# Ten early places instead of eight for the key and value cache, two of them in the space of transposed k

## The chip, the cores and the metric

The kernel runs on one core of a Trainium2 chip. The metric is device time in microseconds of one launch. A second number, the span, is the time from the first to the last instruction in a profiled execution.

## What is computed

One layer of a decoder in float32, for a prompt of 1024 tokens and for 8 sequences that each get 4 new tokens behind 2048 cached ones. Only the part on the sampled sequences matters here: attention of their 4 new tokens over the cached keys and values, with three dilations whose windows are (128,1), (512,4) and (2048,16).

```python
k_all = jnp.concatenate([k_buf.astype(k.dtype), k], axis=1)
v_all = jnp.concatenate([v_buf.astype(v.dtype), v], axis=1)
stats = [dilated_branch_sample(q, k_all, v_all, w, d) for w, d in DILATED_CFG]
...
mixed = jnp.concatenate([rms_norm(y_a, g_norm_a), rms_norm(y_b, g_norm_b)], axis=-1) @ w_out
```

For a sequence this touches the last 512 cached rows (the near keys) and 4 of every 16 rows of the first 1536 (the far keys), and its own 4 rows. After it come an output projection, a layer norm and a mixture of experts.

## The kernel before

The stages run one after the other, each in a block of its own with a barrier at the end: front, attention (the prompt's), sampling, mixing (normalisation and output projection), experts, finish. Buffers are placed by hand at addresses, and every order is written out by hand with semaphores; each engine runs its own list.

In `attention`, SyncE first loads modulation weights, then the first eight pieces of the cache: four near pieces of k into ring0["slots"] (L1104), four far ones into ring0["far"] (L1110), between copies of the cache to the output (L1089). Its last waits, at the end of its list, are for those copies and for the modulation rows in DRAM (L1120, L1121).

In `sampling`, eight sequences are taken in two groups g of four. The cache comes in 32 pieces: 16 of k, then 16 of v. In each 16 the order is group 0 near (4 sequences), group 0 far, group 1 near, group 1 far. A near piece is 1 MB (128 partitions, 8 KB each), a far piece 0.75 MB (96 partitions, 8 KB each, from rows 32 KB apart). They go round a ring of RING = 10 places; piece n goes to place n % 10 once the reader of piece n - 10 has passed (`consumed`). Places 0 to 7 are ring0's, 8 and 9 are ring1. SyncE issues them in order (`load`, L1415 near, L1417 far).

TensorE has 16 units u of k, eight per group (units 0 to 3 and 8 to 11 are near, the others far). For each unit it turns k (`turn`, L1456), in two halves that ScalarE and VectorE copy out of PSUM (`evict`), then makes the scores of the unit before (`scores`, L1470). The own keys come last in a group (`own_scores`). VectorE masks a group (`mask`, L1625), ScalarE takes the exponential, TensorE turns the weights (`turn_weights`), and sums the values (`values`, L1512): part 0 of a group uses near pieces, part 1 far ones. `select` (L1526) gathers the result. In between, VectorE and ScalarE normalise the prompt's rows (`row_sums`, `scale`, `lower`, `upper`), which split them in a high and a low half for the output projection. When the ring's pieces in places 2 and 3 have been read for the last time, SyncE loads half of w_out over them (L1431); `mixing` loads the other half as its first DMA (L1856).

The order of the last part of TensorE's list:

```python
values(0, 0)
for r in range(3):
    turn_weights(1, r)
values(0, 1)
values(1, 0)
select(0)
values(1, 1)
select(1)
```

Of the kernel before, what the change touches and what calls it, by code (L numbers as in the profile page):

```python
# [23 lines left out]
F32 = mybir.dt.float32  # L24
# [6 lines left out]
P = 128  # L31
D = 1024
KD = D // P
SEQ = 1024
# [101 lines left out]
def program(nc, a, out, dram):  # L136
    ctx = ExitStack()
    with ctx:
# [6 lines left out]
        silu = sb("silu", [P, KD, NSEQ])  # L145
        s_ring0 = [Sem(nc.alloc_semaphore(f"ring{j}"), 16) for j in range(8)]
        s_wo = [Sem(nc.alloc_semaphore(f"wo{j}"), 16) for j in range(4)]
# [5 lines left out]
        with ExitStack() as late:  # L153
            sbl = alloc(late)
            at_a = aligned(nc.sbuf_base)
            gelu_in = sbl("gelu_in", [P, CT, TOK])
            ssq = sbl("ssq", [P, NT + 1, CT])
            with ExitStack() as c2:
                sb2 = alloc(c2)
                at_q = aligned(nc.sbuf_base)  # L160
                qT = sb2("qT", [P, PAIRS, TOK])
                kT = sb2("kT", [P, PAIRS, TOK])
                at_v = aligned(nc.sbuf_base)
                v = sb2("v", [P, NT + 1, DB])
                front(nc, a, out, dram, ident, cols, silu, gelu_in, ssq, qT, kT, v, at_q, at_v, s_cache)
                at_b = aligned(nc.sbuf_base)
                ybT = sb2("ybT", [P, PAIRS, TOK])
                at_r = aligned(nc.sbuf_base)
                ring0 = {"at": at_r, "slots": sb2("ring0", [P, 4, 4, DB]),
                         "at_far": aligned(nc.sbuf_base), "far": sb2("ring_far", [P, 4, 4, DB]),  # L170
                         "wo": nc.alloc_sbuf_tensor_at("wo_early", [P, 4, D], F32, offset=at_r + 2 * 16 * DB)}
                attention(nc, a, out, dram, ident, silu, qT, kT, v, ybT, ring0, s_ring0)
                split = {n: nc.alloc_sbuf_tensor_at(n, [P, CT, TOK], F32R, offset=at)
                         for n, at in (("yah", at_q), ("ybh", at_q + 4 * CT * TOK), ("yal", at_a), ("ybl", at_b))}
                sampling(nc, a, ident, qT, kT, v, gelu_in, ybT, ssq, at_v, split, ring0, s_ring0, s_wo)
                mixing(nc, a, out, dram, ident, cols, gelu_in, ybT, ssq, logits, at_v, split, ring0, s_wo, s_rows)
# [839 lines left out]

def attention(nc, a, out, dram, ident, silu, qT, kT, v_all, ybT, ring0, s_ring0):

# [7 lines left out]
    with ExitStack() as ctx:  # L1026
# [22 lines left out]
        s_cp = S("a_cp", 16)  # L1049
        s_cT = S("a_cT")  # L1050
        s_mw = [S(f"a_mw{p}", 16) for p in range(RING)]
        s_mb = S("a_mb", 16)
# [30 lines left out]
        def _(sp):  # L1083
# [36 lines left out]
            sp.wait_ge(s_cp.sem, s_cp.at(B - CT + 2))  # L1120
            sp.wait_ge(s_mo.sem, s_mo.at(GROUPS * QUAD))  # L1121

        @block.gpsimd
        def _(pool):
            nc.gpsimd.memset(mbias[:, :, :], 0.0).then_inc(s_mz.sem, s_mz.unit)
            nc.gpsimd.memset(cT[:, :, :], 0.0).then_inc(s_cT.sem, s_cT.unit)
            pool.wait_ge(s_cT.sem, s_cT.at(1))
            nc.gpsimd.tensor_copy(cT[:, :, 0:NSEQ], silu[:, :, :]).then_inc(s_cT.sem, s_cT.unit)

        @block.tensor  # L1130
# [179 lines left out]

def sampling(nc, a, ident, qT, kT, v_all, ya, ybT, ssq, at_v, split, ring0, s_ring0, s_wo):

    G = B // 4
    KT_ = 8
    RING = 10
    PIECES = 8 * 2 * G
    NPC = 4 * 2 * G
    NW = 4
    with ExitStack() as ctx:
# [4 lines left out]
        S = lambda n, unit=1: Sem(new_sem(n), unit)  # L1324
        ring1 = sb("s_ring", [P, RING - 8, 4, DB])
        wo = ring0["wo"]
# [3 lines left out]
        qz = sb("s_qz", [P, B, PAIRS, NS])  # L1330
        kown = sb("s_kown", [P, PAIRS, NS])
        bias = sb("s_bias", [P, SKEYS])
# [17 lines left out]
        s_b = S("s_b", 16)  # L1350
        s_ring = [*s_ring0, *(S(f"s_r{j}", 16) for j in range(8, RING))]
        s_z = S("s_z")
        s_q = S("s_q")
        s_own = S("s_ownc")
        s_tp = S("s_tp")
# [33 lines left out]
        ROUNDS = ((0, 1, 2, 3), (4, 5, 6, 7), (8,))  # L1389
        early = (ring0["slots"], ring0["far"], ring1)  # L1390
        slot = lambda n: early[n % RING // 4][:, n % RING % 4, :, :]
        k_piece = lambda g, h, c: 8 * g + 4 * h + c
# [13 lines left out]
        @block.sync  # L1406
        def _(sp):
            sp.dma_start(bias[:, :], a["k_sbias"][:, 0, :]).then_inc(s_b.sem, s_b.unit)

            def load(n):  # L1410
                if n >= RING:
                    s, value = consumed(n - RING)
                    sp.wait_ge(s.sem, s.at(value))
                if n // 4 % 2 == 0:
                    sp.dma_start(slot(n), rows_of(n)[PAST - NEAR:PAST, :].rearrange("(p i) n -> p i n", i=4)).then_inc(s_ring[n % RING].sem, s_ring[n % RING].unit)  # L1415
                else:
                    sp.dma_start(slot(n)[0:FARM], rows_of(n)[0:PAST - NEAR, :].rearrange("(m i) n -> m i n", i=16)[:, 0:4, :]).then_inc(s_ring[n % RING].sem, s_ring[n % RING].unit)  # L1417

            for n in range(8, PIECES):
                if n == 8:  # L1420
                    sp.dma_start(own[:, :], a["k_own"]).then_inc(s_in.sem, s_in.unit)
                    sp.dma_start(sel[:, :, :], a["k_sel"]).then_inc(s_in.sem, s_in.unit)
                if n == 18:
                    sp.wait_ge(s_lg.sem, s_lg.at(1))
                    sp.dma_start(bias[:, :], a["k_sbias"][:, 1, :]).then_inc(s_b.sem, s_b.unit)
                load(n)
            s, value = consumed(v_piece(0, 1, 3))
            sp.wait_ge(s.sem, s.at(value))
            w = a["w_out"].rearrange("(k p) n -> p k n", p=P)
            for i in range(NW):  # L1430
                sp.dma_start(wo[:, i, :], w[:, CT + i, :]).then_inc(s_wo[i].sem, s_wo[i].unit)  # L1431
# [12 lines left out]
        def _(pe):  # L1444
# [29 lines left out]
            def own_scores(g):  # L1474
                pe.wait_ge(s_own.sem, s_own.at(1))
                lo = SKEYS - NS
# [95 lines left out]
        def _(act):  # L1572
# [7 lines left out]
            def upper(x, c):  # L1580
                act.wait_ge(s_ma.sem, s_ma.at(2 * CT * x + 2 * c + 2))
                if x == 0 and c == 0:
                    act.wait_ge(s_q.sem, s_q.at(1))
                    act.wait_ge(s_own.sem, s_own.at(1))
                src, dst = ((ya, yah), (ybT, ybh))[x]
                nc.scalar.copy(dst[:, c, 0:SEQ], src[:, c, 0:SEQ]).then_inc(s_hi.sem, s_hi.unit)

            nc.scalar.copy(kown[:, :, :], kT[:, :, SEQ:TOK]).then_inc(s_own.sem, s_own.unit)
            for u in range(KT_ * G):
# [20 lines left out]
        def _(v):  # L1610
# [92 lines left out]
            for u in range(KT_ * G):  # L1703
# [3 lines left out]
                if 2 <= u <= 4:  # L1707
                    add_squares(u - 2)
                if 5 <= u < 5 + CT:
                    scale(0, u - 5, first)  # L1710
                if u == KT_:
                    row_sums(1)
                    mask(0)
                if KT_ + 1 <= u < KT_ + 1 + CT:
                    lower(0, u - KT_ - 1)
                if u == KT_ + 2:
# [1295 lines left out]
```

## Time and profile before

| what | us |
|---|---|
| median of 3 runs | 1340.67 |
| lowest and highest run | 1338.21, 1344.5 |
| the profiled execution | 1340.65 |
| its span | 1338.7 |
| TensorE busy (matmul) | 1196.7 (89% of the span) |
| VectorE busy | 733.9 (55%) |
| ScalarE busy | 576.5 (43%) |
| sampling stage, from its first instruction to the next stage's | 491.7 to 591.1 |

TensorE is the busiest engine over the whole span. The share is a mean over stages with different limits, so for one stage windows, timelines and DMA landings have to be read. PE is TensorE, DVE VectorE, ACT ScalarE, POOL GpSimd, SPq the queue of SyncE. PEclk is the granted clock of TensorE as a share of full speed.

### The profile page before, as it was taken

What the parts mean: (1) busy time and instruction counts of PE and PEld (TensorE: products, weight loads), DVE (VectorE), ACT (ScalarE), POOL (GpSimd) and SP (SyncE); (2) the same over time, 40 slices, a digit from 0 to 9 for tenths busy, and PEclk for the clock granted to TensorE, in tenths of its full rate; (3) what the DMA queues carried; (4) which work ended last, traced back from release to release, by engine and by line L of the source; (5) the groups of instructions that cost most, each with busy time, mean ns of one, the idle gap of its engine ahead of it and who ended that gap; (6) DMA issues with size and microseconds to landing.
All of it is one profiled execution on the core that took longest, in us unless ns stands there. A gap on an engine that the chain in (4) does not pass through costs nothing. (4 is left out here: it accounts for less than half of the span.)

```text
span 1338.7 us, 20995 instructions
## 1 busy us (share of the span) xinstructions
PE 1196.7 (89%) x6981; PEld 905.5 (68%) x6982; DVE 733.9 (55%) x1248; ACT 576.5 (43%) x845; POOL 136.1 (10%) x128
## 2 busy tenths in 40 slices
PE   5999899999799988779993499999999999999885
PEld 3799777876355667337872377787778877777751
DVE  3457524433456756435545685789641454477237
ACT  3655532111355554222333165687531454466124
POOL 0000000000000000003331200011000000001055
PEclk8999889999899999879996599999999999999987
DMA  9998921269769948975325585999661355698464
GB/s 336 363 321 282 331 71 58 79 206 313 275 221 374 321 154 272 295 216 178 123 100 190 181 322 217 359 384 387 230 238 63 120 216 213 235 329 311 178 248 161
DMA packets 102029, 316.95 MB, mean 237 GB/s; under 512 B 12845, under 2 KB 21533, under 8 KB 95290
## 3 DMA queue, kind: packets, MB, share of 16 engines
q1 hardware_dynamic: 85354, 274.25, 58.7%
q0 software_dynamic: 6432, 23.33, 4.8%
q10 hardware_dynamic: 10176, 18.49, 3.7%
q8 instruction: 41, 0.67, 0.2%
q14 instruction: 26, 0.21, 0.0%
HBM read 281.22 MB, written 101.93 MB: 286 GB/s over the span
## 5 line engine op out<-in xcount | busy, mean ns | idle before, releaser
L2621 DVE TENSOR_TENSOR e_downl<-e_wd,e_downh 128x1024 fp32r<-128x1024 f32 x64 | 74.1, 1219 | 62.5 <-ACT e_downh L2516 62.5
L2688 PE MATMUL e_psY<-e_downh,e_hTh 128*128 128x512 f32 x216 | 91.9, 426 | 15.9 <-DVE e_hTl L2642 10.2
L2516 ACT CAST e_downh<-e_wd 128x1024 fp32r<-128x1024 f32 x64 | 62.4, 1046 | 64.6 <-DMA e_wd<-in_w_exp_down 64.4
L571 PE MATMUL n_psA<-n_wh,u_h 128*128 128x512 f32 (+1 forms) x216 | 88.2, 408 | 0.4 <-DVE n_wl L835 0.4
L2688 PE MATMUL e_psG<-e_gateh,e_xTh 128*128 128x512 f32 x216 | 86.5, 400 | 2.0 <-DVE e_gatel L2615 2.0
L2688 PE MATMUL e_psG<-e_uph,e_xTh 128*128 128x512 f32 x216 | 87.8, 406 | 0.2 <-issue 0.2
L2689 PE MATMUL e_psY<-e_downh,e_hTl 128*128 128x512 f32 x216 | 86.7, 402 | 0.0
L2690 PE MATMUL e_psY<-e_downl,e_hTh 128*128 128x512 f32 x216 | 86.6, 401 | 0.0
L573 PE MATMUL n_psA<-n_wh,u_l 128*128 128x512 f32 (+1 forms) x216 | 85.9, 398 | 0.0
L2689 PE MATMUL e_psG<-e_gateh,e_xTl 128*128 128x512 f32 x216 | 85.9, 398 | 0.0
L2690 PE MATMUL e_psG<-e_gatel,e_xTh 128*128 128x512 f32 x216 | 85.9, 398 | 0.0
L572 PE MATMUL n_psA<-n_wl,u_h 128*128 128x512 f32 (+1 forms) x216 | 85.5, 396 | 0.0
L2689 PE MATMUL e_psG<-e_uph,e_xTl 128*128 128x512 f32 x216 | 85.3, 395 | 0.0
L2690 PE MATMUL e_psG<-e_upl,e_xTh 128*128 128x512 f32 x216 | 85.3, 395 | 0.0
L2615 DVE TENSOR_TENSOR e_gatel<-e_wg,e_gateh 128x1024 fp32r<-128x1024 f32 x64 | 74.1, 1220 | 17.0 <-ACT e_gateh L2509 17.0
L2521 ACT CAST e_xTh<-e_psT 128x512 fp32r<-128x512 f32 x56 | 32.7, 585 | 112.5 <-PE e_psT L2683 106.7
L2615 DVE TENSOR_TENSOR e_upl<-e_wu,e_uph 128x1024 fp32r<-128x1024 f32 x64 | 74.0, 1217 | 0.6 <-ACT e_uph L2509 0.5
L2509 ACT CAST e_gateh<-e_wg 128x1024 fp32r<-128x1024 f32 x64 | 62.3, 1047 | 13.2 <-issue 13.2
L2626 DVE TENSOR_TENSOR e_xTl<-e_psT,e_xTh 128x512 fp32r<-128x512 f32 x56 | 38.6, 688 | 48.6 <-ACT e_xTh L2521 48.6
L2509 ACT CAST e_uph<-e_wu 128x1024 fp32r<-128x1024 f32 x64 | 62.4, 1049 | 5.6 <-DMA e_wu<-in_w_exp_up 5.5
L2688 PEld LDWEIGHTS e_psY<-e_downh,e_hTh 128*128 128x128 f32 x216 | 41.6, 193 | 26.4 <-DVE e_downl L2621 13.7
L2589 POOL COPY e_ids<-ids 128x1 int32 (+1 forms) x28 | 15.6, 556 | 416.3 <-PE e_psT L2683 412.0
(417 smaller groups left out, 2600.0 us busy)
## 6 DMA issues: line engine op xcount, KB each, us to landing
e_wg<-in_w_exp_gate SPq DMA_DIRECT2D x16, 2048.0 KB
e_wu<-in_w_exp_up SPq DMA_DIRECT2D x16, 2048.0 KB
e_wd<-in_w_exp_down SPq DMA_DIRECT2D x16, 2048.0 KB, 14.9
out_k_s<-in_cache_win_k SPq DMA_DIRECT2D x8, 4088.0 KB, 24.1
out_v_s<-in_cache_win_v SPq DMA_DIRECT2D x8, 4088.0 KB, 34.0
a_wring<-in_w_ada SPq DMA_DIRECT2D x16, 1024.0 KB, 5.2
scratch_y<-e_y ACTq DMA_DIRECT2D x54, 256.0 KB, 5.6
n_wr<-in_w_in SPq DMA_DIRECT2D x20, 512.0 KB, 10.6
```

The source lines that it names most:

```text
L571: nc.tensor.matmul(dst, lh, rh, start=(k == 0), stop=False)
L572: nc.tensor.matmul(dst, lh, rl, start=False, stop=False)
L573: last = nc.tensor.matmul(dst, ll, rh, start=False, stop=(k == KD - 1))
L2509: nc.scalar.copy(w[name][H_][:, k:k + 2, :], ew[name][:, k:k + 2, :]).then_inc(s_wh.sem, s_wh.unit)
L2516: nc.scalar.copy(w["down"][H_][:, k, :], ew["down"][:, k, :]).then_inc(s_dh.sem, s_dh.unit)
L2521: nc.scalar.copy(xT[H_][:, par, 4 * half:4 * half + 4, :], psT[:, :, :]).then_inc(s_xh.sem, s_xh.unit)
L2615: nc.vector.tensor_tensor(w[name][L_][:, 2 * i:2 * i + 2, :], ew[name][:, 2 * i:2 * i + 2, :], w[name][H_][:, 2 * i:2 * i + 2, :], ALU.sub ...
L2621: nc.vector.tensor_tensor(w["down"][L_][:, k, :], ew["down"][:, k, :], w["down"][H_][:, k, :], ALU.subtract).then_inc(s_dl.sem, s_dl.unit)
L2626: nc.vector.tensor_tensor(xT[L_][:, par, blocks, :], psT[:, :, :], xT[H_][:, par, blocks, :], ALU.subtract).then_inc(s_tc.sem, s_tc.unit)
L2688: nc.tensor.matmul(dst, left[H_], right[H_], start=first, stop=False)
L2689: nc.tensor.matmul(dst, left[L_], right[H_], start=False, stop=False)
L2690: return nc.tensor.matmul(dst, left[H_], right[L_], start=False, stop=last)
```

## The change

The ring has 12 places. Places 8 and 9 lie in the space of kT, the transposed keys of the prompt, which nobody reads after the attention's last scores; each takes two of its four pairs. Pieces 8 and 9 (k of group 1, near) are loaded at the end of SyncE's list in the attention, each behind a wait on the scores that read that half of kT. The own keys, which sampling needs of kT, are copied to a buffer k_own by GpSimd in the attention, not by ScalarE in sampling. Places 10 and 11 are the old ring1. The high half of the attention's rows (ybh) is written to the same space as places 8 and 9, so the first of its casts waits for the value pieces there. w_out waits for a later reader, since places 2 and 3 now end with pieces 26 and 27. On VectorE, the first mask goes ahead of the row sums, the fourth scaling of the first half moves from unit 8 to unit 9, and the four subtractions start one unit later.

```diff
@@ attention @@
+            sp.wait_ge(s_kown.sem, s_kown.at(1))
+            for i in range(2):
+                sp.wait_ge(s_s.sem, s_s.at(2 * chunk0[STEPS // 2 * (i + 1)]))
+                rows = a["cache_win_k"][4 + i].rearrange("s h d -> s (h d)")[PAST - NEAR:PAST, :]
+                sp.dma_start(ring0["in_k"][i][:, :, :], rows.rearrange("(p i) n -> p i n", i=4)).then_inc(s_ring0[8 + i].sem, s_ring0[8 + i].unit)
...
+            nc.gpsimd.tensor_copy(kown[:, :, :], kT[:, :, SEQ:TOK]).then_inc(s_kown.sem, s_kown.unit)
@@ sampling @@
-    RING = 10
+    RING = 12
...
-            for n in range(8, PIECES):
-                if n == 8:
+            for n in range(10, PIECES):
+                if n == 10:
...
-                if n == 18:
+                if n == 20:
                     sp.wait_ge(s_lg.sem, s_lg.at(1))
...
-            s, value = consumed(v_piece(0, 1, 3))
+            s, value = consumed(v_piece(1, 0, 3))
             sp.wait_ge(s.sem, s.at(value))
...
-                    act.wait_ge(s_own.sem, s_own.at(1))
+                if x == 1 and c == 0:
+                    act.wait_ge(s_pv.sem, s_pv.at(2))
...
-            nc.scalar.copy(kown[:, :, :], kT[:, :, SEQ:TOK]).then_inc(s_own.sem, s_own.unit)
...
-                if 5 <= u < 5 + CT:
-                    scale(0, u - 5, first)
                 if u == KT_:
+                    mask(0)
                     row_sums(1)
-                    mask(0)
-                if KT_ + 1 <= u < KT_ + 1 + CT:
-                    lower(0, u - KT_ - 1)
+                if u in (5, 6, 7, 9):
+                    scale(0, (5, 6, 7, 9).index(u), first)
+                if KT_ + 2 <= u < KT_ + 2 + CT:
+                    lower(0, u - KT_ - 2)
```

## Rows read from the trace of the kernel before

**Rows 1.** Windows: length, busy us (count) of each engine, PEclk, DMA share, GB/s

```profile
480.00:490.00 10.00, 7.87 (x105) 6.77 (x101) 3.22 (x8) 3.43 (x8) 0.00 (x0) 1.00 0.01 2
...
562.00:578.00 16.00, 10.22 (x42) 2.59 (x40) 3.68 (x5) 0.00 (x0) 0.00 (x0) 0.79 1.01 219
...
566.00:570.00 4.00, 3.62 (x20) 0.99 (x24) 0.00 (x0) 0.00 (x0) 0.00 (x0) 0.50 1.04 225
```

**Rows 2.** Timeline of PE in sampling: start, us, instruction, idle before and its releaser

```profile
522.77 0.63 PE L1470 MATMUL s_psS<-s_kTs,s_qz 128*32 128x128 f32 x13 [0.97 <-DVE s_mn L1625]
525.69 0.84 PE L1470 MATMUL s_psS<-s_kTs,s_qz 128*32 128x128 f32 x19 [2.28 <-issue]
...
546.80 0.25 PE L1479 MATMUL s_psS<-s_kown,s_qz 128*32 128x32 f32 x2 [2.81 <-issue]
...
555.27 3.64 PE L1512 MATMUL s_psO<-ring,s_pT 96*32 96x512 f32 x32
...
561.77 1.05 PE L1512 MATMUL s_psS<-ring_far,s_kTs 128*32 128x512 f32 x2 [0.89 <-DMA ring_far<-in_cache_win_v]
566.38 6.36 PE L1512 MATMUL s_psS<-ring_far,s_kTs 128*32 128x512 f32 x26 [3.56 <-DMA ring_far<-in_cache_win_v]
...
580.34 1.06 PE L1512 MATMUL s_psS<-ring,s_kTs 96*32 96x512 f32 x1 [2.33 <-DMA ring<-in_cache_win_v]
...
588.48 1.47 PE L1526 MATMUL s_psS<-s_sel,s_om 128*128 128x32 f32 x8 [0.94 <-DVE s_om L1681]
```

**Rows 3.** Issues of pieces 14-15, then 22-23: ns and start us, us to landing

```profile
L1417 SPq DMA_DIRECT2D ring_far<-in_cache_win_k x2: 312/368/425, 515.1 to 515.4; - x2
DMA to landing us min/median/max: 5.8/7.9/10.0
...
L1417 SPq DMA_DIRECT2D ring<-in_cache_win_v x2: 312/370/427, 541.1 to 541.5; - x2
DMA to landing us min/median/max: 10.0/11.5/13.0
```

**Rows 4.** The same of pieces 24-25, 26-27, 28-31, and SPq's issue at unit 11

```profile
L1415 SPq DMA_DIRECT2D ring_far<-in_cache_win_v x2: 427/428/430, 542.0 to 542.4; - x2
DMA to landing us min/median/max: 14.8/15.8/16.8
...
L1415 SPq DMA_DIRECT2D ring_far<-in_cache_win_v x2: 328/380/433, 554.3 to 554.6; - x2
DMA to landing us min/median/max: 7.5/9.6/11.7
...
L1417 SPq DMA_DIRECT2D s_ring<-in_cache_win_v x2: 428/428/428, 555.1 to 555.6; - x2
L1417 SPq DMA_DIRECT2D ring<-in_cache_win_v x2: 312/370/428, 559.0 to 559.3; - x2
...
DMA to landing us min/median/max: 14.8/17.9/21.0
...
530.93 0.80 SPq L1415 DMA_DIRECT2D s_ring<-in_cache_win_v  x2
```

**Rows 5.** SyncE's last wait in the attention, and the last scores there

```profile
L1121 SPq EVENT_SEMAPHORE  x1: 17/17/17, 480.6 to 480.6; - x1
...
473.80 1.13 PE L1140 MATMUL a_psS<-kT,qT 64*128 64x512 f32 x4
```

**Rows 6.** Timelines of SPq and ACT around the end of sampling

```profile
559.80 1.85 SPq L1431 DMA_DIRECT2D wo_early<-in_w_out  x4
591.14 1.75 SPq L1856 DMA_DIRECT2D x_wo_rest<-in_w_out  x4
...
555.75 3.88 ACT L1586 CAST ybh<-ybT 128x1024 fp32r<-128x1024 f32 x4
```

**Rows 7.** Timeline of DVE: the last subtraction of the first half, unit 15's eviction

```profile
535.59 1.22 DVE L1672 TENSOR_TENSOR yal<-gelu_in,yah 128x1024 fp32r<-128x1024 f32 x1
...
541.80 0.96 DVE L1618 COPY s_kTs<-s_psK 128x768 f32<-128x768 f32 x1 [1.31 <-PE s_psK L1456]
```

More of the change, by code:

```diff
@@ L145, in program @@
         silu = sb("silu", [P, KD, NSEQ])
-        s_ring0 = [Sem(nc.alloc_semaphore(f"ring{j}"), 16) for j in range(8)]
+        s_ring0 = [Sem(nc.alloc_semaphore(f"ring{j}"), 16) for j in range(10)]
         s_wo = [Sem(nc.alloc_semaphore(f"wo{j}"), 16) for j in range(4)]
@@ L165, in program @@
                 front(nc, a, out, dram, ident, cols, silu, gelu_in, ssq, qT, kT, v, at_q, at_v, s_cache)
+                at_k = at_q + 4 * PAIRS * TOK
+                kown = sb2("k_own", [P, PAIRS, NS])
                 at_b = aligned(nc.sbuf_base)
@@ L170, in program @@
                          "at_far": aligned(nc.sbuf_base), "far": sb2("ring_far", [P, 4, 4, DB]),
-                         "wo": nc.alloc_sbuf_tensor_at("wo_early", [P, 4, D], F32, offset=at_r + 2 * 16 * DB)}
-                attention(nc, a, out, dram, ident, silu, qT, kT, v, ybT, ring0, s_ring0)
+                         "wo": nc.alloc_sbuf_tensor_at("wo_early", [P, 4, D], F32, offset=at_r + 2 * 16 * DB),
+                         "in_k": [nc.alloc_sbuf_tensor_at(f"ring_k{i}", [P, 4, DB], F32, offset=at_k + 2 * i * 4 * TOK) for i in range(2)]}
+                attention(nc, a, out, dram, ident, silu, qT, kT, kown, v, ybT, ring0, s_ring0)
                 split = {n: nc.alloc_sbuf_tensor_at(n, [P, CT, TOK], F32R, offset=at)
                          for n, at in (("yah", at_q), ("ybh", at_q + 4 * CT * TOK), ("yal", at_a), ("ybl", at_b))}
-                sampling(nc, a, ident, qT, kT, v, gelu_in, ybT, ssq, at_v, split, ring0, s_ring0, s_wo)
+                sampling(nc, a, ident, qT, kown, v, gelu_in, ybT, ssq, at_v, split, ring0, s_ring0, s_wo)
                 mixing(nc, a, out, dram, ident, cols, gelu_in, ybT, ssq, logits, at_v, split, ring0, s_wo, s_rows)
@@ L1015, in _, with attention @@
                     nc.vector.tensor_copy(strow[:, :], psX[0:NTAIL, :]).then_inc(s_tr.sem, s_tr.unit)
-def attention(nc, a, out, dram, ident, silu, qT, kT, v_all, ybT, ring0, s_ring0):
+def attention(nc, a, out, dram, ident, silu, qT, kT, kown, v_all, ybT, ring0, s_ring0):
     FIRST = 2 * D // MW
@@ L1050, in attention @@
         s_cT = S("a_cT")
+        s_kown = S("a_kown")
         s_mw = [S(f"a_mw{p}", 16) for p in range(RING)]
@@ L1308, in _, with sampling @@
             divisor(STEPS - 1)
-def sampling(nc, a, ident, qT, kT, v_all, ya, ybT, ssq, at_v, split, ring0, s_ring0, s_wo):
+def sampling(nc, a, ident, qT, kown, v_all, ya, ybT, ssq, at_v, split, ring0, s_ring0, s_wo):
     G = B // 4
     KT_ = 8
-    RING = 10
+    RING = 12
     PIECES = 8 * 2 * G
@@ L1324, in sampling @@
         S = lambda n, unit=1: Sem(new_sem(n), unit)
-        ring1 = sb("s_ring", [P, RING - 8, 4, DB])
+        ring1 = sb("s_ring", [P, RING - 10, 4, DB])
         wo = ring0["wo"]
@@ L1350, in sampling @@
         s_b = S("s_b", 16)
-        s_ring = [*s_ring0, *(S(f"s_r{j}", 16) for j in range(8, RING))]
+        s_ring = [*s_ring0, *(S(f"s_r{j}", 16) for j in range(10, RING))]
         s_z = S("s_z")
         s_q = S("s_q")
-        s_own = S("s_ownc")
         s_tp = S("s_tp")
@@ L1389, in sampling @@
         ROUNDS = ((0, 1, 2, 3), (4, 5, 6, 7), (8,))
-        early = (ring0["slots"], ring0["far"], ring1)
-        slot = lambda n: early[n % RING // 4][:, n % RING % 4, :, :]
+        places = [*(ring0["slots"][:, i, :, :] for i in range(4)), *(ring0["far"][:, i, :, :] for i in range(4)),
+                  *(r[:, :, :] for r in ring0["in_k"]), *(ring1[:, i, :, :] for i in range(RING - 10))]
+        slot = lambda n: places[n % RING]
         k_piece = lambda g, h, c: 8 * g + 4 * h + c
@@ L1474, in own_scores @@
             def own_scores(g):
-                pe.wait_ge(s_own.sem, s_own.at(1))
                 lo = SKEYS - NS
```

1 line of the change is left out of this document (removed).

## The prediction, made before the change was run

> **What bounds the kernel now.** The table of engines and the forty slices say that TensorE is busy nearly everywhere. The change lies in one stage, sampling, so I cut the span into short windows around it [rows 1]. Two things stand out. From 480 to 490 us, the last ten microseconds of the attention, the DMA engines do nothing (share 0.01, 2 GB/s). From 562 to 578 us they are full (1.01) and TensorE works 10.22 of 16 us. Then I read TensorE's own timeline there [rows 2]: from 559.8 us on it sums the values of the second group of four sequences, and stops four times for a piece of the cache; the rows show 0.89, 3.56 and, as the last, 2.33 us. That one ends at 580.34, when piece 31, the last of 32, lands. What follows it is a fixed tail: the rest of the products, the sums of the last block, a scaling on VectorE, the selecting product at 588.48, and the next stage's first DMA at 591.14, 10.8 us in all [rows 2, 6]. So the landing of piece 31 sets the end of the stage, and everything later waits for it.
>
> Next I asked what sets that landing. The landing times of the pieces give it [rows 3, 4]. A piece lands at its issue plus its time to landing: 22 and 23 at 551.1 and 554.5, 24 and 25 at 556.8 and 559.2, 26 and 27 at 561.8 and 566.3, 28 at 569.9 and 31 at 580.3. They come one after another without a pause, so the queue is the bound and not the issue. The steps show two prices. A near piece (1 MB, 128 partitions) behind another costs 2.4 us. A far piece (0.75 MB in 96 partitions) costs 3.4 to 3.6, though it is smaller: (580.3 - 569.9) / 3 = 3.5. A near piece with far ones behind it costs 566.3 - 561.8 = 4.5.
>
> **The change part by part.**
>
> *Two more places in the space of k.* Pieces 8 and 9 are issued in the attention, behind everything that SyncE has there. SyncE leaves its last wait at 480.6 us and the last scores that read k run at 473.8 to 474.9 [rows 5], so neither of the two added waits on the scores, nor that on the copy, holds it. The first lands like one on an idle queue, at most 5.8 us (that of a far piece [rows 3]), the second a near step of 2.4 later: by 489, inside the idle stretch and ahead of sampling at 491.7. Cover: that stretch; without it they would cost the 4.8 us that they cost now.
>
> *All later loads go two pieces earlier.* Each piece n now waits for what piece n - 12 held. Pieces 12 to 15 are issued near 502, 16 to 19 near 515, 20 to 23 when unit 11 has been turned, 24 to 27 when unit 15 has been turned, 28 to 31 when the first half of the first group's values is done. In the trace these moments are 530.9, 541.1 to 542.0 and 554.3 [rows 3, 4]. The queue has by 530.9 nothing left: 12 to 15, four far pieces, take it to 502 + 5.8 + 4.5 + 2 x 3.4 = 519, and 16 to 19 need 4 x 2.4 us more. From there I add up. Far pieces 20 to 23: 5.8 us for the first on an idle queue, 4.5 for the second (515.4 + 10.0 less 515.1 + 5.8), and 3.4 each for two more [rows 3]: 548.0. Near pieces 24 to 27, issued well before that: 3 x 2.4 + 4.5 = 11.7, so 559.7. Far pieces 28 to 31, issued before that too: 3.6 + 3 x 3.5 = 14.1, so 573.8. That is 6.5 us ahead of 580.3. Bounds: with every far piece at 3.4 and every near one at 2.4, 530.9 + 5.8 + 3 x 3.4 + 4 x 2.4 + 4 x 3.4 = 570.1, a gain of 10.2. If only the transfer of two near pieces leaves the busy stretch, 2 x 2.4 = 4.8. I take 6.5, because it uses for each neighbour of pieces the step of the same pair in the trace.
>
> TensorE reaches the last four pieces earlier, so it does not become the bound: values of the second group begin about 559.8 as now (558.9, where the rows' products end, and those of the new tokens) and no longer stop: 3.64 us for 32 products, as the group from 555.27 shows [rows 2]. The selecting product takes about 1, and from 564.5 on it waits for pieces 29, 30, 31. That wait is longer than the present ones, so the clock is again at its lower level (0.50 from 566 to 570, after a stop of 3.56 us [rows 1, 2]) and the tail stays 10.8 us.
>
> *Weights w_out.* They reuse places 2 and 3, which now hold pieces 26 and 27, so their four DMAs wait for the second group's near values: about 563.5 instead of 559.8 [rows 6]. They stand behind piece 31 in the queue anyway: 2 MB are two near pieces, 4.8 us, so they land at 578.6. The next stage needs them at 591.5 - 6.5 = 585. Zero, with 6 us of margin. If it were late, each microsecond would count whole.
>
> *The copy of k's own columns* leaves ScalarE, where a wait for TensorE followed it, for an idle GpSimd early in the attention: zero, at worst some tenths.
>
> *ybh written into k's space.* ScalarE's four casts, 3.88 us from 555.75 [rows 6], must wait for values that end at 558.9, so they end at 562.8. Two of VectorE's four subtractions (1.22 us each [rows 7]) follow, then the first group's result near 565, then the other two: about 567.5, before the last products. Zero; cover is the wait for piece 31.
>
> *Mask before row sums, one scaling later.* In unit 8 VectorE masks earlier. TensorE waited 0.97 us for it at 522.77, so 1.0 is the most that can come. But 13 products later it stands for 2.28 us with nothing that the profile shows as a reason [rows 2]. I read both this and the 2.81 us ahead of 546.80 as waits for instructions. If so, an earlier arrival is waited away. I take 0 of 0 to 1.0. In unit 13 VectorE gets one more subtraction of 1.22 us, with only 1.31 us of slack by unit 15 [rows 7]; the turn of unit 15 may slip 0.6 to 1.0 us. The loads that hang on it stand in a queue full until 548, so zero.
>
> The Trainium skill weighs on two of these steps, and the sum does not use it. By "DMA: Bandwidth & Descriptors", section "Bandwidth", 16 MB move at 425 GB/s. The near pieces agree (1 MB in 2.4 us), the far ones don't (0.75 MB in 3.5 us). By that rate a far piece would cost an estimated 1.9 us and the queue would never bind again. That is the first rival below, and the rows speak against it. "Runtime: NRT & Kernel Launch", section "Instruction fetch mechanics", says that instructions come by DMA in blocks of 256 and that this is mostly hidden. The trace has two unexplained waits of 2.3 and 2.8 us where the DMA engines are full, so here it isn't hidden. The second and third rivals rest on the rows for it.
>
> Sum: -6.5 us of 1340.65 (profiled execution; span 1338.7, median of the runs 1340.67): 1334.1.
>
> **Rivals.** *The queue is faster than I say.* Piece 31 lands at 570.1 and TensorE's clock stays high: 10.2, and the tail is shorter: its products take 7.2 us now (580.34 to 588.48 less 0.94) and at full clock about 3.64 less the four made ahead, with 0.9 for the new tokens, 4.1; selecting some 0.4 less. Together 10.2 + 3.1 + 0.4 = 13.7, 1327.0. For it: the 3.4 and 2.4 are measured. Against: every stretch with near and far pieces mixed shows more. Without any DMA bound the values would end near 569 and the stage near 572.5, 18.6 earlier, 1322. 12% for both.
>
> *Instruction waits eat it.* The queue now is four pieces deep where it was two, and before 530.9 it is full in stretches where it was not. A wait of 2.3 to 2.8 more, once or twice before unit 11 is turned, moves the whole chain of loads: gain 1 to 4, 1338. For it: the two waits seen [rows 2]; against: their number depends on where block ends fall. 23%.
>
> *Slower.* The same mechanism at each block of instructions between 491.7 and 530.9, about four: 4 x 2.8 = 11.2 against 6.5, so 4.7 slower, 1345.4. It decides from the third wait on (8.4 over 6.5), and with low clock behind each wait (3.1 us a half of values) passes 0.5%. 7% for slower at all, 5% past 0.5%.
>
> *It does nothing,* because the loads in the attention are not issued before its end, or the queue was not the limit: 1340.7. The 480.6 [rows 5] and the landings without a pause [rows 4] speak against. 5%.
>
> **How the numbers follow.** The forecast has 53%. Its own range is 1332 to 1337. The range of 8 in 10 takes in the bound of 10.2 with 1.0 from the mask (11.2, 1329.5) and some scatter of the runs below it, the instruction waits and the case of no effect above. It leaves out the first rival (12%) and the slower one (7%): 1328.5 to 1341.0. About 0.5%, 6.7 us, can be told from no change. That line lies inside my forecast, so it splits it: faster by more 47% (a little over half of the forecast's 53%, the first rival, and the part of the steps with 1.0 from the mask), within 48%, slower 5%.
>
> **What would show it.** Right: pieces 8 and 9 issued at 480.7 and landed by 488; 20 to 23 issued near 531 and all landed near 548; no stop of TensorE in the second group's near values; piece 31 at 573 to 575; the next stage's first DMA near 584.6 with w_out there since 579; the rest of the kernel shifted as a whole. Wrong: unexplained waits of TensorE before 531 longer than 2.3 us in sum, far pieces landing 4 us apart, or a later stage that gives the time back.

## The result and the profile after

| | before | changed |
|---|---|---|
| median of 9 runs each | 1340.67 us | 1328.3 us |
| lowest to highest | 1335.45 to 1344.5 | 1324.19 to 1333.6 |
| ratio, 95% interval | | 0.992, 0.99 to 0.9941 |
| profiled execution, its span | 1340.65, 1338.7 | 1328.28, 1326.3 |

The change makes the kernel 0.8% faster, 10.7 us by the ratio, where 6.5 was forecast. The first question is whether that time comes from sampling. I cut each span at the first DMA of each stage, as SyncE's timeline shows them:

| us | up to attention | attention | sampling | mixing | experts | finish | span |
|---|---|---|---|---|---|---|---|
| before | 339.0 | 152.7 | 99.4 | 130.3 | 560.8 | 56.5 | 1338.7 |
| changed | 338.2 | 155.1 | 88.9 | 130.4 | 557.3 | 56.3 | 1326.3 |

Sampling gives 10.5. The rest nearly cancels (-0.8, +2.4, +0.1, -3.5, -0.2), and it is scatter: over the 14 profiled kernels of this study the attention took 151.7 to 156.1 us and the experts 556.7 to 560.8, in no order that fits their edits. So I read only the stage, and in time from its own start: 491.7 us before [rows 1 to 6], 493.35 changed. (Lengths of stages and parts are differences of times rounded to 0.1 us, so their last digit can be off by one.)

SyncE's timeline of the changed kernel in sampling (start, us, instruction, tiles, count):

```profile
483.39 0.83 SPq L1130 DMA_DIRECT2D ring_k<-in_cache_win_k  x2
493.35 0.33 SPq L1417 DMA_DIRECT2D s_bias<-in_k_sbias  x1
...
530.36 0.80 SPq L1426 DMA_DIRECT2D ring_k<-in_cache_win_v  x2
...
542.20 1.77 SPq L1424 DMA_DIRECT2D ring<-in_cache_win_v  x4
552.42 1.74 SPq L1426 DMA_DIRECT2D ring_far<-in_cache_win_v  x4
561.73 1.77 SPq L1440 DMA_DIRECT2D wo_early<-in_w_out  x4
582.28 1.75 SPq L1864 DMA_DIRECT2D x_wo_rest<-in_w_out  x4
```

The first line is the new one, pieces 8 and 9. Unit 11's release (530.36) answers to 530.93 in [rows 4], the last line to 591.14 in [rows 6]. The landings of pieces 8-9, 20-21, 22-23, 24-27 and 28-31 (ns of the issues, their starts, then us to landing):

```profile
L1130 SPq DMA_DIRECT2D ring_k<-in_cache_win_k x2: 368/396/423, 483.4 to 483.8; - x2
DMA to landing us min/median/max: 4.9/5.9/6.9
...
L1426 SPq DMA_DIRECT2D ring_k<-in_cache_win_v x2: 328/378/427, 530.4 to 530.7; - x2
DMA to landing us min/median/max: 5.7/7.0/8.3
...
L1426 SPq DMA_DIRECT2D s_ring<-in_cache_win_v x2: 393/616/838, 531.2 to 531.7; - x2
DMA to landing us min/median/max: 12.2/13.5/14.8
...
L1424 SPq DMA_DIRECT2D ring<-in_cache_win_v x4: 346/430/435, 542.2 to 543.5; - x4
DMA to landing us min/median/max: 6.5/9.8/14.5
...
L1426 SPq DMA_DIRECT2D ring_far<-in_cache_win_v x4: 328/424/426, 552.4 to 553.7; - x4
DMA to landing us min/median/max: 8.9/13.2/17.7
```

Start plus time to landing: pieces 8 and 9 are there at 488.3 and 490.7, before the stage starts. Piece 23 lands at 531.7 + 14.8 = 546.5, piece 27 at 543.5 + 14.5 = 558.0 and piece 31 at 553.7 + 17.7 = 571.4, where it was 580.3 [rows 4]. TensorE's timeline of the changed kernel, with the same columns and the idle time before in brackets:

```profile
525.11 0.85 PE L1479 MATMUL s_psS<-s_kTs,s_qz 128*32 128x128 f32 x19 [1.00 <-issue]
...
540.76 0.60 PE L1479 MATMUL s_psS<-s_kTs,s_qz 128*32 128x96 f32 x17 [1.38 <-issue]
...
546.60 0.25 PE L1487 MATMUL s_psS<-k_own,s_qz 128*32 128x32 f32 x2 [1.54 <-issue]
...
564.60 1.04 PE L1520 MATMUL s_psS<-ring_far,s_kTs 96*32 96x512 f32 x2 [0.92 <-DMA ring_far<-in_cache_win_v]
567.86 1.92 PE L1520 MATMUL s_psS<-ring_far,s_kTs 96*32 96x512 f32 x2 [2.22 <-DMA ring_far<-in_cache_win_v]
571.46 6.38 PE L1520 MATMUL s_psS<-ring_far,s_kTs 96*32 96x512 f32 x26 [1.69 <-DMA ring_far<-in_cache_win_v]
...
579.77 1.31 PE L1534 MATMUL s_psS<-s_sel,s_om 128*128 128x32 f32 x8 [0.94 <-DVE s_om L1689]
```

These answer to [rows 2]. The 0.97 for the mask is gone, and 2.28 and 2.81 with nothing as their reason are now 1.00 and 1.54, with a new one of 1.38. All three waits for data are for far pieces, 3.3 to 3.6 us apart; the near values no longer stop. The chain is as before: TensorE waits for the landing of the last piece, and from there to the next stage it takes 582.28 - 571.46 = 10.8 us, the same 10.8.

| us | before | changed |
|---|---|---|
| stage start to unit 11's release | 39.2 | 37.0 |
| release to the first use of piece 31 | 49.4 | 41.1 |
| to the next stage's first DMA | 10.8 | 10.8 |

### The profile page after: what moved, and what is told of

Read it like the earlier page. It is cut to its first block and busy times, and to the rows that moved or that the text cites. A ratio compares the mean times of both kernels' runs of the same rounds, so it can differ in the third digit from the quotient of the medians.

```text
span 1326.3 us, 20996 instructions
## 1 busy us (share of the span) xinstructions
PE 1191.3 (90%) x6981; PEld 903.1 (68%) x6982; DVE 735.7 (55%) x1248; ACT 575.8 (43%) x844; POOL 135.3 (10%) x129
## 5 line engine op out<-in xcount | busy, mean ns | idle before, releaser
L2696 PE MATMUL e_psY<-e_downh,e_hTh 128*128 128x512 f32 x216 | 90.9, 421 | 14.3 <-DVE e_hTl L2650 9.7
L2517 ACT CAST e_gateh<-e_wg 128x1024 fp32r<-128x1024 f32 x64 | 62.4, 1047 | 13.2 <-issue 13.2
L1223 DVE CUSTOM_DVE_ANT_0 lg<-a_psS,bias 128x512 f32<-128x512 f32 (+3 forms) x96 | 49.3, 551 | 13.8 <-DMA bias<-in_k_bias 11.3
## 6 DMA issues: line engine op xcount, KB each, us to landing
n_wr<-in_w_in SPq DMA_DIRECT2D x20, 512.0 KB, 10.6
```

What stands on the lines that cost most here:

```text
L1223: nc.vector.tensor_tensor_reduce(out=lg[:, s % 3, hh, 512 * c:512 * c + m], in0=psS[:, hh, k % 2, 0:m], in1=bias[:, lo:lo + m], scale=-0.1 ...
L2517: nc.scalar.copy(w[name][H_][:, k:k + 2, :], ew[name][:, k:k + 2, :]).then_inc(s_wh.sem, s_wh.unit)
L2696: nc.tensor.matmul(dst, left[H_], right[H_], start=first, stop=False)
```

## Experiments

The parts can be separated: the order on VectorE, the two places, and the loads in the attention. Times with an interval are ratios to the kernel before on the same chip, with the 95% interval. Four kernels ran only once and have a time alone, beside the median of the kernel before on their chip. Stage lengths are from one profile each. In the diffs `...` stands for lines left out, and the `.then_inc(...)` behind a DMA is left out too.

**The order alone** (before, with only the lines of VectorE's order changed):

```diff
                 if u == KT_:
+                    mask(0)
                     row_sums(1)
-                    mask(0)
...
-                    scale(0, u - 5, first)
+                    scale(0, (5, 6, 7, 9).index(u), first)
```

> The kernel before with only VectorE's new order (mask ahead of row sums, fourth scaling one unit later). The sampling stage took 99.4 us before and 89.0 after. Queue theory: the loads that TensorE releases at unit 11 may come up to 1.0 us earlier, by the wait for the mask that goes; piece 31 still ends the stage, so the stage takes 98.4 to 99.4 us. Rival, that the order brings all of the 2.3 us by which the release came earlier: 97.1 us. Device time 1338 to 1340.7.

Ratio 0.9998 (0.9976 to 1.002), stage 102.5 us. TensorE's timeline of this kernel:

```profile
524.83 1.49 PE L1470 MATMUL s_psS<-s_kTs,s_qz 128*32 128x128 f32 x19 [3.87 <-issue]
```

The mask's 0.97 is gone and the unexplained wait is 3.87 where it was 2.28: what arrived earlier was waited away, and TensorE goes on 34.4 us into the stage, where it was 34.0 before. The clock in the 6 us from 524 on was 0.52. That makes this profile's stage longer than the 98.4 to 99.4 expected; the total doesn't show it. The order buys nothing by itself.

**Everything but the order** (changed kernel with the old order):

```diff
                 if u == KT_:
-                    mask(0)
                     row_sums(1)
+                    mask(0)
```

> The changed kernel with VectorE's old order. Queue theory: the stretch from the release at unit 11 to the landing of piece 31 stays 41 us (49.4 before), the release comes 0 to 2.3 us later than in the changed kernel: stage 89.0 to 91.3 us, device time 1328 to 1331. Rival, that the order matters more than the places: stage over 93 us.

Ratio 0.9925 (0.9902 to 0.9947), stage 88.8. That is the whole gain without the order. Its TensorE shows the mask's wait again and no stop of the other kind in that unit:

```profile
523.34 1.31 PE L1479 MATMUL s_psS<-s_kTs,s_qz 128*32 128x128 f32 x32 [0.97 <-DVE s_mn L1633]
```

Unit 11 is released 529.05 - 492.2 = 36.9 us into the stage, as in the changed kernel. So the 2.2 us won before unit 11 aren't the order's either. Behind the release piece 31 takes the 41.1 us that it takes in the changed kernel.

**The early load alone** (changed kernel, but each later piece n waits again for what piece n - 10 held):

```diff
-    RING = 12
+    RING = 10
...
+        slot = lambda n: ring0["in_k"][n - 8][:, :, :] if n in (8, 9) else places[n % RING]
```

> The changed kernel, but with a ring of 10 as before: pieces 8 and 9 are loaded into the space of k in the attention, and pieces 18, 19, 28, 29 go to the old ring1, each behind the same reader as before. Queue theory: the queue still has two near and eight far and four more near pieces to load behind unit 11, so the early load by itself gives nothing: stage 97 to 99.4 us. Rival, that the transfer taken out of the stage is what helps, wherever it was: 4.8 us, 94.6 or less, down to 89.

Ratio 0.9997 (0.9976 to 1.0018), stage 97.6. Unit 11 is released 37.2 us in, and the use of piece 31 comes 49.6 after it, as before. **The places alone** (pieces 8 and 9 loaded in sampling):

```diff
-            for i in range(2):
-                sp.wait_ge(s_s.sem, s_s.at(2 * chunk0[STEPS // 2 * (i + 1)]))
...
-            for n in range(10, PIECES):
-                if n == 10:
+            for n in range(8, PIECES):
+                if n == 8:
```

> The changed kernel, but pieces 8 and 9 are issued as sampling's first pieces and not in the attention; the 12 places stay. Queue theory: 4.8 us more of transfers stand ahead of piece 12, the queue has no idle stretch left before unit 11, and piece 31 lands 2.5 to 4.8 us later than in the changed kernel: stage 91.5 to 93.8 us. Rival, that only the number of places counts: 89 us.

Ratio 0.9942 (0.9918 to 0.9967), stage 93.3: release 39.9 in, piece 31 used 43.6 later. By the ratios the early load alone is worth 0.4 us, the places alone 7.8, and both without the order 10.0; by the stages 1.8, 6.1 and 10.6. The places carry it. What the early load adds to them, 2.3 us by the ratios, is inside the intervals; the stages show it in two parts.

The first part lies behind the release. In places alone piece 31 is used 2.5 us later behind it than in the changed kernel, because the queue hasn't run dry when unit 11 releases the next loads. The windows around the release, changed and then places alone (length, busy us and count of each engine, clock, DMA share, GB/s):

```profile
530.00:531.00 1.00, 1.00 (x11) 0.96 (x9) 0.85 (x2) 0.64 (x1) 0.00 (x0) 1.00 0.08 27
...
532.00:534.00 2.00, 2.00 (x37) 1.80 (x30) 2.00 (x3) 0.75 (x1) 0.00 (x0) 1.00 1.03 425
```

Pieces 20 and 21 land 5.7 and 8.3 us behind their issue in the first, 8.3 and 11.2 in the second. The second part lies ahead of the release. Release of unit 11 in us into the stage:

| without the early load | | with it | |
|---|---|---|---|
| before | 39.2 | changed | 37.0 |
| order alone | 41.9 | all but the order | 36.9 |
| places alone | 39.9 | early load alone | 37.2 |

The stops of TensorE in that stretch differ. Before has waits of 0.97 and 2.28, the order alone 3.87, the early load alone 0.18. Places alone has only 1.13 but a low clock without a stop ahead of it, as its window shows:

```profile
516.00:522.00 6.00, 6.00 (x62) 5.42 (x62) 2.56 (x4) 1.74 (x2) 0.00 (x0) 0.56 1.03 217
```

Seven of the 14 kernels have such a stretch, between 22 and 30 us into the stage. In warm_tail (below), whose instructions are the changed kernel's up to there, it stands from 516.74 to 520.74 at 0.57:

```profile
516.74:520.74 4.00, 4.00 (x47) 3.47 (x47) 2.15 (x3) 1.56 (x3) 0.00 (x0) 0.57 0.88 324
```

It has no stop where the changed kernel has 1.22 us of them, but TensorE is busy for 35.8 us up to the release instead of 34.7, and the release comes at 36.9 against 37.0. far_contig gives 36.7. So the eight releases fall in two groups, by the early load. It isn't the only way: before_wide (below), which has no early load but shorter far transfers, has its release at 36.2. far_split, which has the early load and twice as many far transfers, has it at 37.9. What the groups have in common is in the next experiment.

**Are the unexplained waits tied to a place in TensorE's list?** The changed kernel with 64 waits, all met long before, ahead of unit 0:

```diff
+            for _ in range(64):
+                pe.wait_ge(s_ring[0].sem, s_ring[0].at(1))
             for u in range(KT_ * G):
```

> The changed kernel with 64 more waits, already met, in TensorE's list ahead of sampling's first unit. If the unexplained stops of TensorE (0.22, 1.00, 1.38, 1.54 us, behind 15, 13, 15 and 30 products of their blocks) are waits for the next block of instructions, they move by 64 instructions, 32 products with their weight loads, to earlier places in the list. Rival, that they hang on data or semaphores: they stay behind the same products. Time within 2 us of the changed kernel either way.

One run: 1332.52 us (before's median there 1339.32), stage 93.4. TensorE's stops without a reason are now these, and no others:

```profile
496.60 6.33 PE L1465 MATMUL s_psK<-ident,ring 128*128 128x128 f32 x32 [5.09 <-issue]
...
543.78 0.32 PE L1465 MATMUL s_psK<-ident,ring 96*128 96x96 f32 x1 [2.42 <-issue]
```

The stops among the scores and at the new tokens are gone, although data, buffers and the other engines' lists are the same; one stands now inside a turn. (The first holds the added waits themselves, so its 5.09 can't be taken as a price.) The two stops ahead of the release prove little, since they are missing in warm_tail as well. But the three behind it, 1.38, 0.30 and 1.54, stand in warm_tail with the same lengths at the same products, and here all three are gone. So the stops hang on positions in the instruction list. Behind the stop of 2.42 the clock was 0.50 for the window from 544 to 548. The time was expected within 2 us of the changed kernel; one run can't settle that, but the stage is 4.5 us longer. Its release comes 2.9 us later, behind the added waits, and the queue is then full, as in places alone (share 1.07 from 532 to 534), so piece 31 is used 43.7 us behind it.

That they are waits for instructions another view of the traces shows. The DMA queues have one of kind "instruction", with transfers of 16 KB; the view by queue places each in time. Three windows of 0.1 us, from 523.2 in before, 522.8 in the changed kernel and 517.3 in far_wide (packets, MB, share of 16 engines):

```profile
q8 instruction: 1, 0.02, 71.3%
...
q8 instruction: 1, 0.02, 58.6%
...
q8 instruction: 1, 0.02, 68.1%
```

Before's transfer takes 1.13 us to 524.4, and the stop of 2.28 ends at 525.69. The changed kernel's takes 0.95 us to 523.8, and the stop of 1.00 ends at 525.11. Over the 14 kernels there are 28 stops with the releaser "issue" besides those of 0.30 and the 5.09, and each ends 1.3 to 1.7 us after such a transfer has ended. (The stops of 0.30, always ahead of the same scores, have none that close.) The trace doesn't say whose instructions these are; the 28 matches say that they are TensorE's. The transfers take 0.9 to 1.4 us; what makes a stop long is that one starts late. The transfer that the two stops above wait for, in us into the stage:

| | start of the transfer |
|---|---|
| before, order alone, places alone | 31.6, 31.8, 32.3 |
| changed, all but the order, early load alone, warm_tail | 29.5, 29.3, 29.4, 29.3 |
| far_contig, far_split, 64 waits ahead | 27.1, 30.2, 30.9 |
| before_wide, far_128, far_wide, wide_warm | 24.2 each |

The changed kernel, warm_tail and far_128 have the same list of TensorE up to there and have run it without a stop up to 24.2 us. So the start depends on what else the DMA engines carry. With the early load the transfer starts 2.1 us sooner than before, and that is the 2.2 us of the release but for 0.1. That also is why the order buys nothing: the stop ends when the instructions are there, whenever TensorE gets to it. How a queue of cache pieces holds the transfer up no run here shows.

**Why does a far piece cost 3.5 us?** The prediction took this price as given, and piece 31 hangs on it. Theory: its runs of 8 KB lie 32 KB apart. Rival: it goes to 96 partitions, not 128. Two kernels read other rows of the cache for the far pieces, first in 96 partitions without gaps:

```diff
-rows_of(n)[0:PAST - NEAR, :].rearrange("(m i) n -> m i n", i=16)[:, 0:4, :]
+rows_of(n)[0:4 * FARM, :].rearrange("(m i) n -> m i n", i=4)
```

> The changed kernel, but each far piece is read from the first 384 cached rows in one contiguous stretch (still 96 partitions of 8 KB each), so it attends to other keys and values than it should. If a far piece costs 3.3 to 3.5 us because its rows lie 32 KB apart, it now costs about 1.8 (three quarters of a near piece), the queue no longer binds and TensorE doesn't stop for values: stage 79 to 82 us. Rival, that the 96 partitions cost it: far pieces still land 3.3 us apart, stage 89 us.

Then in 128 partitions with gaps, 1 MB instead of 0.75:

```diff
-sp.dma_start(slot(n)[0:FARM], rows_of(n)[0:PAST - NEAR, :].rearrange("(m i) n -> m i n", i=16)[:, 0:4, :])
+sp.dma_start(slot(n), rows_of(n)[0:PAST - NEAR, :].rearrange("(m i) n -> m i n", i=12)[:, 0:4, :])
```

> The changed kernel, but each far piece is read as 128 partitions of 8 KB whose rows lie 24 KB apart (1 MB instead of 0.75), so the keys and values are others than they should be. If the distance costs: 4/3 of 3.4 us, 4.5 us a piece, piece 31 lands some 9 us later, stage 97 us. Rival, that 96 partitions are the cost: 2.4 us a piece as for near ones, stage 80 to 84 us.

Issue and landing of pieces 28-31 in the first, then in the second:

```profile
L1426 SPq DMA_DIRECT2D ring_far<-in_cache_win_v x4: 328/425/426, 554.1 to 555.4; - x4
DMA to landing us min/median/max: 9.0/13.9/18.8
```

```profile
L1426 SPq DMA_DIRECT2D ring_far<-in_cache_win_v x4: 328/430/431, 549.4 to 550.7; - x4
DMA to landing us min/median/max: 7.3/10.6/13.9
```

From the first to the last landing, by three: (574.2 - 563.1) / 3 = 3.7 us without gaps, (564.6 - 556.7) / 3 = 2.6 with gaps and a third more bytes. The theory fell; the partitions are the price. Nor is it the smaller transfer: w_out's four of 0.5 MB, to 128 partitions, stand behind piece 31 in the changed kernel and land 1.3 us apart ((576.3 - 572.4) / 3):

```profile
L1440 SPq DMA_DIRECT2D wo_early<-in_w_out x4: 347/432/434, 561.7 to 563.1; - x4
DMA to landing us min/median/max: 10.7/12.0/13.2
```

Why 96 partitions cost more no run here shows. The stages are 89.9 and 81.1, the times of one run each 1329.93 and 1322.51 (before's median there 1339.32). The window of the second kernel in the middle of these landings:

```profile
560.00:564.00 4.00, 1.60 (x6) 0.14 (x2) 2.25 (x3) 0.00 (x0) 0.00 (x0) 0.95 1.00 416
```

Share 1.00 at 416 GB/s, where it is 1.01 at 219 in [rows 1]. So the share says that the engines are occupied, not how much they move.

**Far pieces in 128 partitions with the right rows.** The last 32 partitions take rows that nobody uses:

```diff
-sp.dma_start(slot(n)[0:FARM], rows_of(n)[0:PAST - NEAR, :].rearrange("(m i) n -> m i n", i=16)[:, 0:4, :])
+sp.dma_start(slot(n), rows_of(n).rearrange("(m i) n -> m i n", i=16)[:, 0:4, :])
```

> The changed kernel, but each far piece that sampling loads is read from all 2048 cached rows, 4 of every 16, in 128 partitions of 8 KB: 1 MB instead of 0.75, the last 32 partitions unused, result unchanged. If the 96 partitions are what makes a far piece slow (3.3 to 3.5 us), it now costs 2.4 to 2.6: 12 pieces from unit 11 on take about 33 us instead of 41, stage 81 to 82 us, device time about 1320. Rival, that the larger transfer costs more than the shape saves: stage 89 or more.

Ratio 0.9861 (0.983 to 0.9893), median 1319.35 beside 1336.24 of before on that chip: the lowest ratio here, 1.4% against the change's 0.8%. Stage 83.6, where 81 to 82 was expected.

```profile
L1426 SPq DMA_DIRECT2D ring_far<-in_cache_win_v x4: 327/430/431, 549.7 to 551.1; - x4
DMA to landing us min/median/max: 7.2/11.0/14.8
...
565.87 6.46 PE L1520 MATMUL s_psS<-ring_far,s_kTs 96*32 96x512 f32 x26 [1.46 <-DMA ring_far<-in_cache_win_v]
...
543.91 0.25 PE L1487 MATMUL s_psS<-k_own,s_qz 128*32 128x32 f32 x2 [0.50 <-issue]
```

3.0 us a piece, more than the 2.4 to 2.6 expected, and of the waits with no releaser only 0.30 and 0.50 are left. **The same edit in the kernel before:**

> The kernel before with far pieces in 128 partitions. Queue theory: the loads behind unit 11 (14 pieces) take about 38 us instead of 49, now partly bound by their issue times (pieces 30 and 31 are issued 28 us behind unit 11), so piece 31 lands 10 to 12 us earlier: stage 87 to 89.5 us, device time 1328 to 1331. So the shape alone would be worth about what the change was. Rival, that the change took the same slack and the shape works only with 12 places: stage over 94 us.

Ratio 0.9913 (0.9881 to 0.9945), stage 87.7, piece 31 used 567.93 - 527.33 = 40.6 us after unit 11's release. The shape alone is worth what the whole change is worth: both shorten the same queue. The two together give 1.4%; whether that is less than 0.9 and 0.8 added the intervals don't tell.

**Far pieces in two parts, 64 and 32 partitions:**

```diff
...
+                    for part in (slice(0, 64), slice(64, FARM)):
+                        sp.dma_start(slot(n)[part], rows[part, 0:4, :])
```

> The changed kernel with each far piece that sampling loads in two DMAs, of 64 and of 32 partitions. If a DMA over 96 partitions is slow by the way in which that number is spread, 64 and 32 should go at the near pieces' rate, 0.75 x 2.4 = 1.8 to 2.5 us a piece, stage 80 to 82 us. Rival, that any transfer to fewer than 128 partitions is slow: still 3.3 us a piece or more, stage 89 us.

```profile
L1429 SPq DMA_DIRECT2D ring_far<-in_cache_win_v x8: 471/528/584, 555.3 to 559.2; - x8
DMA to landing us min/median/max: 6.5/11.3/17.0
```

1332.5 us in one run (before's median there 1336.24), stage 93.6; piece 31 is used at 576.31, 45.0 us behind the release, where the changed kernel has 41.1. The first of the eight lands at 561.8 at the earliest and the last at 576.2: no cheaper than whole. The Trainium skill, "DMA: Bandwidth & Descriptors", section "Rules for kernel authors", asks for 128 partitions and 1 MiB or more per DMA for full bandwidth, and says that two transfers to disjoint halves of the partitions serialize. The 128 partitions agree with these kernels (2.6 to 3.0 us against 3.4 to 3.7); the size doesn't show here, since w_out's 0.5 MB move at about the near pieces' rate. The split into 64 and 32 isn't one in halves, but is no quicker either.

**The tail at full clock.** The 26 products behind piece 31 take 6.38 us, and the window from 572 to 576 shows a clock of 0.50. Idle products fill the waits for pieces 29 to 31:

```diff
+            def warm(n):
+                pe.wait_ge(s_ma.sem, s_ma.at(16))
+                for _ in range(n):
+                    nc.tensor.matmul(psK[:, 0, 0, :], ident[:, :], ident[:, :], start=True, stop=True)
...
+                                if g == 1 and part == 1 and c >= 1:
+                                    warm((6, 11, 12)[c - 1])
```

> The changed kernel with 6, 11 and 12 idle products of 128 columns into free PSUM ahead of TensorE's waits for pieces 29, 30 and 31. If the tail behind piece 31 is long because the clock has fallen (0.50), the time from its landing to the next stage's first DMA falls from 10.8 to about 7.3 us, and the next stage's first products run at full clock too: stage 85.5 us and 2 to 3 us more behind it, device time 1322 to 1325. Rival, that the clock falls all the same or the idle products only delay: stage 89 to 90 us, device time as the changed kernel's or 1 us more.

Ratio 0.9919 (0.989 to 0.9949), stage 87.0, where 85.5 was expected. Its TensorE, one timeline line and two windows:

```profile
571.78 3.62 PE L1527 MATMUL s_psS<-ring_far,s_kTs 96*32 96x512 f32 x26
...
568.00:572.00 4.00, 4.00 (x31) 2.98 (x34) 0.00 (x0) 0.00 (x0) 0.00 (x0) 1.00 0.96 289
...
580.00:584.00 4.00, 1.95 (x11) 1.66 (x12) 2.73 (x3) 4.00 (x5) 0.29 (x2) 0.50 0.81 273
```

The products take 3.62 instead of 6.38, and the tail 579.72 - 571.78 = 7.9 us instead of 10.8 (7.3 expected). At the passage to the next stage the clock is at 0.50 again. The total doesn't show the 2 us of the stage against the changed kernel: the intervals of 0.992 and 0.9919 are wider than that. **Both, with wide far pieces and 2, 10 and 10 idle products** (far_wide's edit, `warm` as above, and other numbers):

```diff
+                                    warm((2, 10, 10)[c - 1])
```

> Far pieces in 128 partitions and 2, 10 and 10 idle products ahead of the waits for pieces 29, 30 and 31 in the changed kernel. The tail behind piece 31 ran at the low clock with far pieces of 128 partitions too (26 products in 6.50 us); at the high clock it is 2.9 us shorter: stage 78 to 79 us, device time about 1317.5. Rival, that the idle products now delay the real ones: stage 81 us or more.

Ratio 0.9882 (0.9847 to 0.9917), stage 83.7: no better than wide alone.

```profile
L1426 SPq DMA_DIRECT2D ring_far<-in_cache_win_v x4: 328/430/432, 546.6 to 547.9; - x4
DMA to landing us min/median/max: 7.0/10.7/14.3
...
559.29 2.50 PE L1509 MATMUL s_psK<-ident 128*128 128x128 f32 x20
...
562.70 2.50 PE L1509 MATMUL s_psK<-ident 128*128 128x128 f32 x20
...
565.13 3.62 PE L1527 MATMUL s_psS<-ring_far,s_kTs 96*32 96x512 f32 x26
```

Piece 31 is there at 547.9 + 14.3 = 562.2, but the products on it start at 565.13. Ten idle products (two records each) take 2.50 us; I had counted them at half of that, and they stood in front of the real ones for 2.9 us. The higher clock gave that back, no more.

## Why the prediction was right, and where its sizes were off

The kernel is faster by the path that was forecast, and by more than was forecast: 10.7 us by the ratio, 10.5 in the stage, against 6.5. The ratio puts it at 1329.9, below the forecast's own 1332 to 1337 and inside the wide range from 1328.5 on; the median of the runs, 1328.3, lies just below that. Two terms of the sum were too small, and both erred the same way.

**What bounds the stage: right.** The landing of piece 31 set the end before and sets it now. The earlier places move it, and everything behind it moves with it. Shorter transfers in the kernel before, with no change of the ring, move it too (before_wide).

**Pieces 8 and 9 in the idle stretch: right.** Issued at 483.4, 2.7 us later than I wrote, since the attention ran longer, and landed in 4.9 and 6.9 us where 5.8 and 8.2 were reckoned. Not foreseen: with this load the instructions ahead of unit 11's release came 2.1 us sooner. The prediction also reckoned that the queue has nothing left by the release. That holds, and it counts: without the early load the queue isn't dry by then, and piece 31 comes 2.5 us later (places alone).

**The sum of steps: right in kind, too large by 1.8 us.** From unit 11's release to piece 31 it had 573.8 - 530.9 = 42.9; measured 41.1:

| pieces | reckoned | measured |
|---|---|---|
| 20 to 23 (far, from the issue) | 17.1 | 16.1 |
| 24 to 27 (near) | 11.7 | 11.5 |
| 28 to 31 (far) | 14.1 | 13.4 |

For pieces 28 to 31 I had taken 3.5 to 3.6 us each; it was 3.3 to 3.6 (3.4 on average). For 20 to 23 I had taken 5.8, 4.5, 3.4 and 3.4, measured were 5.7, 2.9, 4.4 and 3.1: the second step, 4.5, was borrowed from a far piece with near ones behind it, and that was the wrong neighbour.

**The moment of unit 11's release: the term that was mis-sized most.** I took 0 of 0 to 1.0 us; it came 2.2 earlier. The reasoning for zero was about the order, and for the order it holds: 0.9998 alone, and nothing lost without it. The fault was to put the bound of that moment at the mask's 0.97, and to hold the unexplained 2.28 fixed, as if only the order could touch it. It ends when a block of instructions has arrived, and that arrival moved by 2.1 us with the other transfers. Ahead of unit 11's release such waits add up to between 0 and 3.87 us in the kernels here. I had named instruction waits as a rival, but only as one that gets worse. The chance of 23% for it, and the slower rival of the same kind, went in the wrong direction: the sum of unexplained waits in the stage fell from 5.6 us (0.16, 2.28, 0.30, 2.81) to 4.4 (0.22, 1.00, 1.38, 0.30, 1.54).

**What the unexplained waits are: right.** The prediction read them as waits for instructions, and the instruction queue shows it.

**The two terms together:** 6.5 + 1.8 + 2.2 = 10.5, the stage's gain.

**w_out, ybh, the copy of k's own columns: right at zero.** w_out, issued at 561.73, landed by 563.1 + 13.2 = 576.3; I had reckoned 578.6. The casts of ybh now wait for TensorE, as ScalarE's timeline shows, and end at 561.1, ten us ahead of piece 31:

```profile
557.18 3.88 ACT L1595 CAST ybh<-ybT 128x1024 fp32r<-128x1024 f32 x4 [3.18 <-PE s_psO L1520]
```

**The tail: right.** 10.8 us, at the low clock behind the waits; warm_tail shows that 2.9 of it are the clock.

**The rival of a faster queue** had one foot in what happened. Its steps of 3.4 and 2.4 fit the far pieces better than mine (16.0 and 13.6, measured 16.1 and 13.4, mine 17.1 and 14.1), but not the near ones (9.6, measured 11.5, mine 11.7); over the whole stretch the measured 41.1 lies midway between its 39.2 and my 42.9. TensorE's clock did not stay high (0.50 from 572 to 576); it still waited 2.22 and 1.69 us for pieces 30 and 31.

**Open:** how the cache pieces hold up a transfer of instructions; why a low clock came without a stop in some kernels; how often the 2.2 us come (each kernel has one profile); why 96 partitions cost more than 128; and to which instruction each stop belongs, since the 64 added ones moved them by an amount that I can't explain.

## What to carry to other kernels

Where one engine waits for the last piece of a queue, add the steps of its pieces from the moment that releases them, and check whether the queue has run dry at that moment. If it hasn't, a load moved into an idle stretch ahead brings all later ones forward; here it was worth little without the places and, by the stages, more with them. Look at the price of each shape in that queue before its order: here rows to 96 partitions cost more than a third more bytes to 128, and the simple edit of a load was worth as much as the reuse of buffers. And a wait with no releaser is not a constant: look for the instruction queue's transfer ahead of its end, and give it a range in both directions.

## What the runs showed of the hardware that was not expected

- DMAs of 0.75 MB to 96 partitions land 3.4 to 3.7 us apart on average over four in a row, of 1 MB to 128 partitions 2.4 to 3.0, with rows in one piece or 24 or 32 KB apart, and of 0.5 MB to 128 partitions 1.3. In 64 and 32 partitions the same 0.75 MB are no faster. The DMA share reads 1.0 at 219 and at 416 GB/s.
- TensorE's stops without a releaser end 1.3 to 1.7 us after a 16 KB transfer on the instruction queue has ended, in 28 cases; those of 0.30 us are of another kind. They sit at positions in its instruction list, were 0.2 to 3.9 us long, and 0.5 to 0.8 with far pieces of 128 partitions. The transfer itself takes 0.9 to 1.4 us; the same one started 24.2 us into the stage with 128 partitions and 27.1 to 29.5 with 96, under the same list of TensorE. The Trainium skill, "Runtime: NRT & Kernel Launch", section "Instruction fetch mechanics", calls the cost of crossing a block boundary mostly hidden; in these stages it is not.
- Ten idle 128 x 128 products of f32 took 2.5 us. They held the clock at 1.00 through waits for data, and it was at 0.50 again behind the passage to the next stage. A low clock also came without a stop ahead of it: 0.56 from 516 to 522 us with TensorE busy all the time (places alone), 0.57 over 4 us in warm_tail.
